# Convolution taps in pairs with other work between them, launch sums behind the key tiles, and a closing sum by shares

## The reference, cut to what matters

```python
def rmsnorm(x, g):
    return x * lax.rsqrt(jnp.mean(x * x, axis=-1, keepdims=True) + EPS) * g

# first block, beginning
mem_n = rmsnorm(mem, mem_norm)
h = rmsnorm(x, mix_norm[0])
mem_k, mem_v = split(mem_n @ w_mem_kv[0])        # 256 columns each
q_mem = (h @ a_in[0])[..., 3 * MAIN_WIDTH:]

# second block, feed-forward; the 256 tokens are an image of 4 x 64
a, val = _split(modulate(_rms_norm(x, norm2_g)) @ w_up, (2816, 2816))
a = conv3x3_per_channel(a.reshape(4, 64, 2816), conv_w) + conv_b
x = x + g2 * ((gelu(a, approximate=False) * val) @ w_down)

return _rms_norm(x, final_norm_g)
```

## Time and profile before

| | |
|---|---|
| median of 3 runs | 1162.6 us (1162.23 to 1165.48) |
| the profiled execution's own time | 1162.78 us |
| its span | 1161.5 us |
| TensorE matmul busy | 1136.4 us (98%), 8982 instructions |
| VectorE busy | 842.8 us (73%) |
| ScalarE busy | 622.1 us (54%) |
| GpSimd busy | 152.0 us (13%) |
| mean DMA rate | 191 GB/s |

### The profile page before, as it was taken

One profiled execution on the slowest core, in us unless ns is written; L12 is line 12 of the kernel. 1 busy time (PEld: TensorE's weight loads), 2 busy tenths in 40 slices (PEclk: granted clock), 3 DMA queues, 4 the chain that ended last, 5 costly groups with the idle time before them and its releaser, 6 DMA issues.

```text
span 1161.5 us, 21863 instructions
## 1 busy us (share of the span) xinstructions
PE 1136.4 (98%) x8982; PEld 1095.3 (94%) x8982; DVE 842.8 (73%) x1312; ACT 622.1 (54%) x944; POOL 152.0 (13%) x111
## 2 busy tenths in 40 slices
PE   7999999999999999999999999999999998999997
PEld 6989999999998899999999898988999998999996
DVE  5767678878875767777777775687546788777766
ACT  5655544344666655444444664755447465455453
POOL 0002210010100003101001000000000033444441
PEclk9999999999999999999999999999999998999999
DMA  8645578776544344888878645354235543555540
GB/s 321 227 155 173 175 241 277 246 244 204 186 140 148 127 162 151 286 273 281 268 262 292 207 161 172 129 174 162 92 109 169 193 165 128 182 182 182 184 162 37
DMA packets 60323, 221.51 MB, mean 191 GB/s; under 512 B 6720, under 2 KB 6976, under 8 KB 59840
## 3 DMA queue, kind: packets, MB, share of 16 engines
q1 hardware_dynamic: 59760, 218.53, 56.6%
q10 hardware_dynamic: 288, 1.05, 0.2%
q0 software_dynamic: 176, 0.52, 0.1%
HBM read 219.03 MB, written 1.05 MB: 189 GB/s over the span
## 4 chain that ended last, share of the span: by engine, by line
PE 86%; DVE 9%; ACT 3%; issue 1%; DMA 1%; SPq 0%; ACTq 0%; DVEq 0%
PE PS L372 24%; PE PS L374 23%; PE PS L373 23%; PE PS L377 15%; DVE w_lo L1391 2%; DVE PS L2028 2%; ACT w_hi L879 2%; DVE ARENA L1424 1%; DMA ARENA<-memT 1%; DVE SQ L1424 0%; DVE H_lo L1434 0%; ACT ARENA L976 0%; PE PS L629 0%; DVE Y_lo L1430 0%; DVE ARENA L2073 0%
## 5 line engine op out<-in xcount | busy, mean ns | idle before, releaser
L1391 DVE TENSOR_TENSOR w_lo<-raw,w_hi 128x1024 fp32r<-128x1024 f32 x324 | 397.9, 1231 | 162.8 <-ACT w_hi L879 162.3
L879 ACT ACTIVATE w_hi<-raw 128x1024 fp32r<-128x1024 f32 x356 | 371.6, 1054 | 134.2 <-PE PS L374 107.6
L372 PE MATMUL PS<-Y_hi,w_hi 128*128 128x256 f32 x1208 | 347.1, 287 | 8.7 <-DVE Y_lo L1430 3.8
L373 PE MATMUL PS<-Y_lo,w_hi 128*128 128x256 f32 x1208 | 342.9, 284 | 0.0
L374 PE MATMUL PS<-Y_hi,w_lo 128*128 128x256 f32 x1208 | 342.9, 284 | 0.0
L372 PEld LDWEIGHTS PS<-Y_hi,w_hi 128*128 128x128 f32 x1208 | 232.5, 192 | 14.3 <-issue 5.8
L373 PEld LDWEIGHTS PS<-Y_lo,w_hi 128*128 128x128 f32 x1208 | 232.8, 193 | 0.4 <-issue 0.2
L374 PEld LDWEIGHTS PS<-Y_hi,w_lo 128*128 128x128 f32 x1208 | 232.7, 193 | 0.0
L372 PE MATMUL PS<-H_hi,w_hi 128*128 128x256 f32 x768 | 220.1, 287 | 1.7 <-DVE w_lo L1391 0.9
L373 PE MATMUL PS<-H_lo,w_hi 128*128 128x256 f32 x768 | 217.3, 283 | 0.0
L374 PE MATMUL PS<-H_hi,w_lo 128*128 128x256 f32 x768 | 217.2, 283 | 0.0
(11 more groups left out here) (256 smaller groups left out, 1424.9 us busy)
## 6 DMA issues: line engine op xcount, KB each, us to landing
raw<-stream SPq DMA_DIRECT2D x404, 512.0 KB, 4.1
ARENA<-memT SPq DMA_DIRECT2D x2, 512.0 KB, 7.7
X<-xT SPq DMA_DIRECT2D x1, 1024.0 KB, 11.4
ARENA<-ctxT SPq DMA_DIRECT2D x1, 1024.0 KB, 5.9
ARENA<-memT SPq DMA_DIRECT2D x1, 1024.0 KB, 8.1
outT<-ARENA SPq DMA_DIRECT2D x2, 512.0 KB, 2.6
CROW<-c_rows SPq DMA_DIRECT2D x1, 512.0 KB, 10.3
ARENA<-c_rows SPq DMA_DIRECT2D x1, 512.0 KB, 12.2
```

The lines of the kernel that those rows point to most:

```text
L372: pe.matmul(o, wh, xh, start=start, stop=False, skip_group_check=True)
L373: pe.matmul(o, wh, xl, start=False, stop=False, skip_group_check=True)
L879: act.activation(w_hi[n % RING][:], raw[at][:], ACT.Copy).then_inc(*mark("hi", n))
L1391: dve.tensor_tensor(w_lo[n % RING][:], raw[raw_of("slot", n)][:], w_hi[n % RING][:], ALU.subtract).then_inc(*mark("lo_dve", n))
```

## The change

It has four parts.

1. **Launch.** The squares of X are shared between ScalarE (chunks 0 to 3) and VectorE (4 to 7), and the squares of the memory go from VectorE to ScalarE. On TensorE both matmul groups of the sum for X stand after the second key slot, those for the memory after the value slots and after the first slot of a_q. The a_q copies, and fills, take new places on ScalarE. 14 in place of 10 matmuls run on constants.
2. **Opening of the convolution stage.** One ScalarE fill moves ahead of the first Gelu, and the second lead tile's image (`lead_conv_gate(1)`) moves from ahead of the norm to behind it. VectorE multiplies lead chunk 0 (`lead_value(0)`) one step earlier.
3. **Convolution loop.** The eight taps go in pairs with the previous chunk's multiplication, a fill, and the previous chunk's G_lo between the pairs. For chunk 1 the multiplication and G_lo, which stood ahead of the taps of chunk 2, now stand between them.
4. **Closing.** Six chunks go by quarters into bank 5, the last two by full matmuls into bank 4, and a matmul with a matrix of 1/32 ("shares") adds the quarters to the same sum. The weight is multiplied into the output beforehand (eight TENSOR_SCALAR), and the norm afterwards (four instructions of 128x512). Four output transfers take the place of two.

```diff
@@ launch, TensorE
             def launch_norms():
+                yield
                 quarters("mix0", CSQ, 5)
+                sum_quarters("mix0", 5)
+                yield
                 yield
                 quarters("mem0")
-                sum_quarters("mix0", 5)
                 yield
                 sum_quarters("mem0")
...
-            for _ in range(10):
+            for _ in range(14):
                 mm(PS[:, 3, 0:T], ONES, consts[:, 0:T])
...
             project_tokens("mem_v0", 256, Y, (6, 7), ("vm0", 1), side)
+            project("a_q", 2, H, lambda i: ("qm", 0, i), side, [norm_low("mix0", k) for k in range(KC)])
             side.finish()
-
-            project("a_q", 2, H, lambda i: ("qm", 0, i), None, [norm_low("mix0", k) for k in range(KC)])
@@ launch, ScalarE
-            squares("mix0", X, None, CSQ)
-            fill()
-            fill()
+            squares_of("mix0", X, CSQ, 0)
+            squares_of("mix0", X, CSQ, 2)
+            fill()
+            fill()
+            squares_of("mem0", MEM, SQ, 0)
             copy_quarters("mix0", 5)
+            squares_of("mem0", MEM, SQ, 2)
             act.wait_ge(*past("init", 0))
             inverse_rms("mix0", b=5)
+            fill()
+            side = Side(norm_his("mix0", H, via=CSQ))
+            side.step(4)
+            squares_of("mem0", MEM, SQ, 4)
+            side.step(2)
+            squares_of("mem0", MEM, SQ, 6)
+            side.finish()
+            fill()
+            fill()
             copy_quarters("mem0")
             fill()
-            side = Side(norm_his("mix0", H, via=CSQ))
-            side.step(5)
-            inverse_rms("mem0")
-            fill()
-            side.finish()
-            fill()
+            to_query = copied(QP, "qm", 0)
+            for i in range(2):
+                to_query(i, AT["a_q"] + i)
+                if i == 0:
+                    inverse_rms("mem0")
+                fill()
@@ convolution stage, ScalarE
             act.preload_act_table(ACT.Gelu)
+            fill()
             conv_value(0)
-            lead_conv_gate(1)
-            fill()
             hidden(2, 0)
             whole(norm_his("norm2", H2, lambda c: SH2(c)))
+            lead_conv_gate(1)
             fill()
             for j in range(LEAD, FC):
                 conv_gate(j)
                 conv_value(j - 1)
-                if j == LEAD:
-                    hidden(2, j - 1)
+                fill()
+                hidden(2, j - 1)
                 fill()
                 fill()
-                if j > LEAD:
-                    hidden(2, j - 1)
-                fill()
@@ convolution stage, VectorE
             lead_scaled(1, up_slot(2, 0))
+            lead_value(0)
             lead_scaled(2, gate_slot(2, 1))
-            lead_value(0)
...
             conv_taps(1)
             fill()
-            lead_value(1)
-            hidden_low(2, 1)
             for j in range(LEAD, FC):
-                if j > LEAD:
+                conv_taps(j, 0, 2)
+                if j == LEAD:
+                    lead_value(1)
+                else:
                     conv_value(j - 1)
+                conv_taps(j, 2, 4)
                 fill()
-                conv_taps(j)
+                conv_taps(j, 4, 6)
+                hidden_low(2, j - 1)
+                conv_taps(j, 6, 8)
                 fill()
-                if j > LEAD:
-                    hidden_low(2, j - 1)
                 fill()
@@ closing, TensorE
-            sum_squares("out")
+            claim(4, 5)
+            for k in range(KC - 2):
+                if k % 2 == 0:
+                    pe.wait_ge(*past("sq", "out", k // 2))
+                row = 32 * (k % 4)
+                last = mm(PS[row:row + 32, 5, 0:T], ONES[:, 0:32], SQ[:, k], k < 4, k + 4 >= KC - 2)
+            last.then_inc(*mark("quarters", "out"))
+            for k in (KC - 2, KC - 1):
+                pe.wait_ge(*past("sq", "out", KC // 2 - 1 if k == KC - 2 else KC // 2))
+                if k == KC - 1:
+                    pe.wait_ge(*past("quartered", "out"))
+                    pe.wait_ge(*past("shares"))
+                    mm(PS[:, 4, 0:T], SHARES, RS[:, 1], False, False)
+                last = mm(PS[:, 4, 0:T], ONES, SQ[:, k], k == KC - 2, k == KC - 1)
+            last.then_inc(*mark("sum", "out"))
@@ closing, VectorE
+            for c in range(KC):
+                if c % 2 == 0:
+                    dve.wait_ge(*past("x_add", 2, c // 2))
+                dve.tensor_scalar(OUT[:, c], X[:, c], gain("final2", c), None, ALU.mult).then_inc(*mark("weighted", c))
             dve.wait_ge(*past("rs", "out"))
-            for c in range(KC):
-                dve.scalar_tensor_tensor(OUT[:, c], X[:, c], gain("final2", c), RS[:, 0], ALU.mult,
-                                         ALU.mult).then_inc(*mark("final", c))
+            dve.wait_ge(*past("weighted", KC - 1))
+            for q in range(KC // 2):
+                two = slice(2 * q, 2 * q + 2)
+                dve.tensor_tensor(OUT[:, two], OUT[:, two], RS[:, 0:1].to_broadcast([P, 2, T]),
+                                  ALU.mult).then_inc(*mark("final", q))
```

49 lines of the change are left out of this document (30 added, 19 removed).

## The result

| | before | after |
|---|---|---|
| median of 4 runs each, us | 1163.38 (1162.23 to 1165.48) | 1156.89 (1156.26 to 1157.35) |
| profiled execution, us | 1162.78 | 1157.14 |
| its span, us | 1161.5 | 1155.8 |
| mean granted clock in it | 0.995 | 0.996 |

What follows compares the result with a forecast made beforehand. TensorE, its matmuls busy 98% of the span, was taken as the bound. Launch -0.7, opening -3.0, closing with end of stage -2.15 sum to -5.85 us on 1162.78: 1156.9, as median 1156.7 us; range 1154.8 to 1159.8.

Steps and rivals of the forecast that it cites:

- The launch: Launch: a_c's first slot starts 0.7 us earlier, after new waits of 1.3 us; bounds -2.0 and +0.5 us.
- The opening: Opening of the convolution stage: first Y_lo 1.4 us earlier, up(4) 3.0 us earlier in all; bounds -4.1 and -1.0 us.
- the term of the low clock: Opening: clock falls again at about 966.8, half speed until 973.0, a chunk's three matmuls then taking 0.72 us.
- Rival A: Opening: clock stays at 2.4 GHz, up(3) waits 1.2 us, -4.1 in place of -3.0, 1155.6 us; chance 0.20.
- Rival B: Opening: new wait for G_lo of chunk 1; opening brings 1.0 us, launch nothing, 1159.4 us; chance 0.13.
- the lower bound: Opening: gain of only 1.0 us if G_lo of chunk 1 comes 2 us later than forecast.
- The loop: Convolution loop, chunks 5 to 20: taps in pairs bring nothing; TensorE's full queue hides the 0.4 us saved on VectorE.
- Rival C: Convolution loop: VectorE's chain becomes the bound; with 0.45 us more a chunk, 1164.8 us; chance 0.05.
- The end of the stage: End of the convolution stage: the stall for G_lo of chunk 20 goes, -0.6 us with its restart.
- The closing: Closing: sum by shares -0.15, products after the norm -0.75, last transfer -0.65 us.
- The last transfer: Closing: 256 KB in place of 512 KB lands in 1.95 us, between bounds 2.6 and 1.3, for 2.6: -0.65 us.
- Rival D: Closing: four transfers in series, each waiting for the one before to land, 1160.6 us; chance 0.04.

Runs made afterwards that it cites:

- taps unbroken: Kernel after, with chunks 3 to 21 running six taps in one run, then G_lo of the previous chunk, then two taps: 1156.68 us, ratio 0.9949.
- late copy: Kernel after, with ScalarE's copy of the quarters behind the last square and TensorE's matmul on the shares last: 1156.21 us, ratio 0.9937.
- launch alone: Kernel before, with only the launch's part of the change: 1162.19 us, ratio 0.9989.
- convolution part alone: Kernel before, with only the convolution stage's part (opening, loop, end of stage): 1158.76 us, ratio 0.9957.
- two transfers: Kernel after, with two output transfers of 512 KB instead of four of 256 KB: 1156.55 us, ratio 0.9942.
- TensorE kept busy: Kernel after, with unread matmuls on constants in the opening, three ahead of the first lead slot and one between its chunks: 1156.72 us, ratio 0.994.
- old loop: Kernel after, with the before's order of taps, fill and G_lo from chunk 2 on, the new opening kept: 1160.64 us, ratio 0.9977.
- closing alone: Kernel before, with only the closing's part (sum by shares, weights ahead of the norm, four transfers): 1162.31 us, ratio 0.9992.
- G_lo earlier: Kernel after, with the copy behind the last square and G_lo of chunk 1 ahead of chunk 2's last four taps: 1155.66 us, ratio 0.9935.

## Why the prediction was right

*What bounds the kernel* stands: TensorE is busy 98% in both, and all that was gained is time in which it stood, or in which it had finished.

*The launch.* -0.81 us for -0.7. Each price came out in the rows: quarters 1.07 us, the bare copy 0.50 for 0.4, 0.6 us lost at the memory's quarters for 0.4, the second sum at 31.62 for 31.5. The warm-up matmuls cost nothing, as they end at 12.33. The +0.19 us at the first product is not from them: TensorE still waits 0.49 us for its weights there.

*The opening.* First Y_lo 1.18 us earlier for 1.4, and then 2.47 us for 1.6. What was off is the term of the low clock, in two ways. Its place: I kept the fall at 966.8, a time of day. Read from the shares of the windows it was at 966.6 before, 2.4 us after the first Y_lo product, and at 964.6 now, 2.2 us after it. More of the half-speed stretch then lay where VectorE's Y_lo set the pace. Its price: I put a chunk's three matmuls at half speed at 0.72 us, where the kernel before has 0.64 (970.72 and 971.36, the first two chunks of its up(2), start 0.64 us apart). Down(0) started at 972.88 (973.5 by the clock of before) instead of at 974.0. Of the 0.76 us by which it came early, counted from the first Y_lo product, the place makes some 0.5 and the price some 0.2.

That the fall came 2.2 us after the product was luck. In the other profiles with this opening it came from 1.2 us (taps unbroken) to 3.8 us (late copy) after it, and in the launch alone 0.6 us ahead of it. It mattered little, because G_lo of chunk 1 holds up(3) in any case: counted from the first Y_lo product up(3) starts at 15.86 or 15.87 us in five profiles (convolution part alone, two transfers, late copy, TensorE kept busy, taps unbroken), and at 16.20 in the kernel after.

*Rival A* (the clock stays up, -4.1 in place of -3.0) did not come in the kernel after, but its price was the better one. It has 24.65 us from the first Y_lo product to up(4); with TensorE kept busy this took 24.59, and up(3) waited 0.83 us for G_lo of chunk 1 (1.2 us by A). What was wrong is its distance to the forecast: the forecast's 25.7 us were 24.84. So at the first addition the clock brought 0.2 us, not 1.1. The Trainium skill, "TensorE: Matmul & The Clock Gate", Part 1, says that activity releases the throttle; the same experiment agrees, with no window under 1.00 in the opening. The old loop's profile has none either, without the added matmuls.

*Rival B*, a new wait for G_lo of chunk 1, was closer than its slack of 1.1 us said. The slack was 0.4 us in the kernel after and gone in four others with its opening (waits of 0.30, 0.96, 0.95 and 0.95 us at up(3): copy late, two transfers, taps unbroken, convolution part alone), in whose profiles the low clock was shorter. It cost none of them time, because the low clock gave what this wait took. The price of B, and of the lower bound, was wrong in its own terms: G_lo 2 us late, less the slack of 1.1, costs 0.9 us and leaves -2.1, not -1.0. The long fill that B feared was there, 2.62 us, but in the kernel before, ahead of G_lo of chunk 2.

*The loop* was right at nothing: G_lo of chunk 2 is done 7.6 us earlier and no chunk waits. *Rival C* needed idling of VectorE to reach TensorE; it did not.

*The end of the stage* -0.72 us for -0.6: the 0.40 us wait of rows 10 is gone.

*The closing* is where a term failed. Products -0.76 us for -0.75: the row of the same operation in another place (rows 4, 0.60 us each) was the right neighbour. The sum by shares brought 0.04 for 0.15. The last transfer brought nothing for 0.65. The step that failed is that the last transfer was priced by itself, as if it had the DMA engines alone: "half the bytes lie between 2.6 and 1.3 us". Their busy share is 0.96 to 1.04 from 1152 to 1155, all four transfers share that stretch, and four go at a lower rate than two (350 and 400 GB/s). The bound of 2.6 us stood in the range. *Rival D*, transfers in series, fell: the four issues take 2.14 us together and the span ends 2.81 us after the last product.

So the total was right partly by luck: the opening gave 0.65 us more than its two terms, and the transfer 0.74 us less. The median fell out right by luck too: its base, 1162.6 us, became 1163.38 with a fourth run, 0.8 us more, and the gain between the medians was 6.5 us, 0.6 more than the sum.

## What to carry to other kernels

Order the follower engine's work by who is waited for: the tile that the bottleneck wants next goes ahead of fills and of chained work, and it need not be wide of it, two or four operations earlier are enough. Before pricing a low clock, ask which engine sets the pace of that stretch. If it is another, the low clock costs nothing there: 3.4 us of half speed within gate(2) left down(0) at 8.98 to 8.99 us from the first Y_lo product (convolution part alone, two transfers, taps unbroken), where the old loop's profile, with no fall, has 8.99 us. Keeping TensorE busy then brings little. And price the end of a kernel by when its bytes start to move and at what rate they all go together: a smaller last transfer does not land sooner while those ahead of it are still on the way.

## What the hardware showed

- The fall of the clock in the opening came for one of three lengths. Adding up what the windows of 1 us from 960 to 976 lack (the share below 1.00, twice), the time at half speed is 6.8 us in four profiles (before, after, launch alone, closing alone), 3.4 us in five (convolution part alone, two transfers, late copy, G_lo earlier, taps unbroken) and none in three, of which only two keep TensorE busy; the third, the old loop, has the same 1.33 us of wait as the kernel after. The interval from the first Y_lo product to the first addition hardly knows it: 181.35 us in the kernel after (6.8 us low), 181.11 and 181.12 with two transfers and the late copy (3.4 us), 181.10 with TensorE kept busy (none). The mean granted clock of the ten runs that keep TensorE busy is 0.998 or 0.999; of 24 runs with the same opening without it (the kernel after, two transfers, late copy, G_lo earlier, taps unbroken) seven reach that, and the others lie from 0.995 to 0.997.
- At half speed the matmuls of 128x256 start every 0.21 us, at full speed every 0.12 us.
- A wait of 2.73 us before up(4) was followed by a second fall in both profiles that have it, one of 2.22 or 2.23 us in neither of the two (before, closing alone). It costs some 1.5 us there, since TensorE sets the pace at that place. Whether the length of the wait decides stays open: these are four profiles.
- Output from SBUF on SyncE's queue: a transfer of 512 KB alone on the DMA engines starts to move 0.8 us after its issue, moves for 1.3 us and has landed at 2.6. Four of 256 KB issued 0.6 us apart landed in 2.3 to 2.7 us each and moved 1.05 MB in 3.0 us; two of 512 KB issued 1.2 us apart did it in 2.6 us.
- A VectorE fill (128x1024) takes 1.22 us in the median; beside a fill of GpSimd's the one ahead of G_lo of chunk 2 took 2.62 and 2.59 us where the two ran together for 1.5 us (before, closing alone), and 1.83 us where it was 0.7 to 0.8 us (launch alone, old loop). That fits with the one drawing out the other; no run sets it apart.
- Eight taps that each wait for the one before take 4.16 us, 0.52 each; a pair with other work behind takes 0.92 us to the next operation's start. The products of two chunks with the norm, 128x512, start every 0.6 us, and eight weight products of 128x256 with one tensor take 2.18 us, 0.27 each, under the bound of 0.35 that rows 14 gave.
